# Scores ahead of up-sums on TensorE, and the dot product ahead of the gate product on VectorE, in two transformer blocks with 16,384 gathered experts

## The chip, the cores and the metric

The kernel runs on one core of a Trainium2 chip. The metric is the device time of that core in microseconds (us), for the whole program: two blocks of a transformer for 512 tokens of width 1024, in float32.

## What is computed

Two blocks follow one another. Each is a mixer (attention-like branches, merged by gates) and then a PEER feed-forward layer. That layer is what fills the time. Cut to what matters here:

```python
def peer_ffn(h, ...):
    q = h @ w_query                          # 8 heads, two halves of 128
    v1, i1 = top_k(q1 @ keys1, 16); v2, i2 = top_k(q2 @ keys2, 16)
    expert_idx, gates = ...                  # top 16 of the pairs, softmax: 8 * 16 = 128 experts a token
    u = take(expert_down, expert_idx)        # a row of 1024 for each token and expert
    act = gelu(einsum('bpd,bphkd->bphk', h, u))
    vv = take(expert_up, expert_idx)         # another row of 1024
    return einsum('bphk,bphkd->bpd', gates * act, vv)
```

The second block's mixer has three attentions (with a forget gate, with a sliding window and sinks, and over a memory of 256 tokens), whose items are scores, softmax and a weighted sum of values:

```python
s = einsum('bqhd,bkhd->bhqk', q_i, k) * scale + bias
p = softmax(where(mask, s, NEG_INF))
o = einsum('bhqk,bkhd->bqhd', p, v)
```

## The kernel before, in words

Tokens stand in tiles of 128, one token on each partition. For each of the 2 layers x 4 tiles x 128 experts, 1024 **slots** in all, one indirect DMA (L243, issued by POOL) gathers 128 rows of 8 KB, one for each token: the expert's down row and up row side by side, 1 MB, into one of 8 buffers (called held_z and held_pair in the profile: four of the buffers lie in the tile z). A slot n then passes through these steps:

- VectorE forms the **dot product** of the down rows with h (L309, a custom operation with a small read of the accumulator behind it) into `dot`.
- For two slots at a time (GROUP = 2), ScalarE makes **gelu** (L282, `bent`), and VectorE the **product of gelu and gate** (L304, `weight`).
- ScalarE makes a **diagonal** of the weight (L289, `diag`, one of 4 tiles), and TensorE multiplies the up rows by it and adds up over a tile's 128 slots in PSUM: the **up-sum** (L263, four matmuls, eight records in the profile).
- The end of the up-sum frees the buffer, and POOL issues the gather of slot n + 8 into it (L241 and L242 wait for `added`).

All this is cut into **beats**. In beat n, VectorE has the dot product of slot n and, for odd n from 3 on, the weights of the pair n - 3 and n - 2; ScalarE has gelu for the pair n - 2 and n - 1 if n is even, then the diagonal of slot n - 3; TensorE has the up-sum of slot n - 4; POOL issues slot n + 4. The order within a beat and engine is that in which the methods `pe`, `act` and `dve` of the class Gather write it (L252 to L329).

The beats run beside all the work that is left once the first tile's experts are chosen (host work, here): each stage takes `beats`, shares them out over its own steps, and calls `beats.pe(pe, step)` and its like on each engine after that step's own work. Host stages are the projections (p2, pg, po: TensorE mostly), head norms (hn), merges (mg), the choice of experts for the next tiles (c, with top-k on VectorE), and the attention stage (`attention_stage`, L843, foxa), which runs once for each half of the tokens. After about 3400 us only the drain is left: beats with nothing beside them.

`attention_stage` runs a software pipeline over N = 40 items, in N + 4 steps. In step s, TensorE has the scores of item s (`score`, L910, for the forget-gate items a second matmul L912) into one of two PSUM tiles, the transposes of item s - 2 (`turn`, L920), the weighted values of item s - 3 (`weigh_values`, L929) and then the step's beats. VectorE has the maximum of item s (`peak`, L984 to L988), which waits for the scores, the division for item s - 1 (`weigh`, L994 to L996), the copy of the result of item s - 4 (`take`, L1001) and then the beats. ScalarE has the exponential of item s (L952), the copy of the transposed item s - 2 (L965) and then the beats. Scores of item s wait until the exponential of item s - 2 has been made, since they use its PSUM tile.

The same function also serves an attention of the first block without beats ("mlaa"); there the order of instructions stays as it was.

Of the kernel before, what the change touches and what calls it, by code (L numbers as in the profile page):

```python
# [9 lines left out]
ALU = mybir.AluOpType  # L10
# [7 lines left out]
TT = S // P  # L18
# [21 lines left out]
NJ = PH * K16  # L40
# [169 lines left out]
class Gather:  # L210
# [85 lines left out]
                act.activation(self.sums[:, u * 512:(u + 1) * 512], self.acc[u][:], ACT.Copy).then_inc(self.kept, 1)  # L296

    def dve(self, dve, n):
        g, s = divmod(n - WEIGH_AT, GROUP)
        if s == 0 and 0 <= g < SLOTS // GROUP:  # L300
            t, q = divmod(g, NJ // GROUP)
            at = slice(q * GROUP, (q + 1) * GROUP)
            dve.wait_ge(self.bent_made, g + 1)
            dve.tensor_tensor(self.weight[:, t % 2, at], self.bent[:, t % 2, at], self.gate[:, t % TT, at], ALU.mult).then_inc(self.weighed, 1)  # L304
        if n < SLOTS:
            t, s = divmod(n, NJ)
            down = self.pair[n % BUFS][:, 0:D]
            dve.wait_ge(self.landed[n % BUFS], 16 * (n // BUFS) + 16)
            ins = dve.tensor_tensor_reduce(down, down, self.hrow[:, t % TT, :], 1.0, 0.0, ALU.mult, ALU.add, self.dot[:, t % 2, s:s + 1])  # L309
            if n % GROUP == GROUP - 1:  # L310
                ins.then_inc(self.dotted, 1)
        for u in range(2):
            t = self.tile_end(n, 3 + 2 * u)
            if t is not None:
# [528 lines left out]
def attention_stage(nc, name, k, items, heads, vdim, oT, sunk_from=None, sinks=None, sunk_T=None, sunk_loads=(), loads=(), saves=(), beats=None, spare=(), fetch=None,  # L843
# [21 lines left out]
    with ExitStack() as stack:  # L865
# [12 lines left out]
        with nc.Block(no_gpsimd_drain=True) as block:  # L878
# [20 lines left out]
            def _(pe):  # L899
# [23 lines left out]
                def weigh_values(n):  # L923
                    vs, (at, size, _, _) = items[n][3], lands(n)
                    pe.wait_ge(copied, n + 1)
                    if n >= 2 or n and not apart(n):
                        pe.wait_ge(taken, n - 1 if apart(n) else n)
                    for j, v in enumerate(vs):
                        last = pe.matmul(po[n % PO][at:at + size, 0:P], v, pT[n % 2][:, j * P:(j + 1) * P],  # L929
                                         start=j == 0, stop=j == len(vs) - 1)  # L930
                    last.then_inc(summed, 1)

                for step in range(N + 4):
                    if step < N:
                        score(step)
                    if 2 <= step < N + 2:
                        turn(step - 2)
                    if 3 <= step < N + 3:
                        weigh_values(step - 3)
                    beats.pe(pe, step)  # L940

            @block.scalar
# [1425 lines left out]
```

## Time and profile before

| | |
|---|---|
| median of 3 runs | 3985.33 us (3980.39 to 3996.19) |
| the profiled execution | 3991.26 us |
| its span, first to last instruction | 3989.4 us |
| first gather issued | 807.82 us |
| PE / DVE / ACT / POOL busy | 77% / 59% / 23% / 29% of the span |
| HBM read | 1256.17 MB, of it 1073.81 MB on the gathers' queue |
| granted TensorE clock, mean | 0.83 |

A row of the profile's windows gives, for a stretch of time in us from the span's start, the busy time of each engine with its number of instructions, then the granted TensorE clock as a share of full speed, the share of the stretch in which the 16 DMA engines were busy, and what they moved in GB/s. A row of waits names who waited, for whom, how long in total, how often, and the longest. In a row of the timeline the number in brackets is the idle time of that engine before the instruction, and what ended it. PE is TensorE, PEld its weight loads, DVE VectorE, ACT ScalarE.

### The profile page before, as it was taken

The page shows a single profiled execution, that of the slowest core. Times are in us where ns is not written, and L with a number is a line of the kernel's source. Part 1 is how long each engine was busy: PE and PEld are TensorE (multiplying, and loading weights), DVE is VectorE, ACT ScalarE, POOL GpSimd, SP SyncE. Part 2 cuts the span into 40 slices and gives each one's busy share as a digit, 9 for nine tenths or more (in the row PEclk, how much of TensorE's full clock was granted, in tenths as well). Part 3 has the DMA queues.
Part 4 walks back from the last instruction along what each step waited for, and adds up shares of the span by engine and source line. Part 5 has one row for each costly group of instructions (what it writes and reads, how often), then busy time and mean ns, then how long its engine had stood idle before and what let it go on. Part 6 is the DMA issues. An engine that isn't in the chain of part 4 may idle for free. (4 is left out here: it accounts for less than half of the span.)

```text
span 3989.4 us, 51160 instructions
## 1 busy us (share of the span) xinstructions
PE 3057.4 (77%) x18686; PEld 1577.7 (40%) x18686; DVE 2370.5 (59%) x6158; ACT 915.4 (23%) x2506; POOL 1152.4 (29%) x1029
## 2 busy tenths in 40 slices
PE   5975596756787765988899865979798876676666
PEld 4853395612354211633455522634465531111111
DVE  6557745476446677457545577457645578655554
ACT  2113232012111112136321111136412111111111
POOL 0000000043333444323323342323333334444442
PEclk8998698867798876977999986969999987766666
DMA  5510002289999999988999997977999999999998
GB/s 214 188 68 1 6 4 93 97 364 400 350 384 372 419 411 393 400 322 309 367 398 373 370 406 269 411 286 264 348 416 376 360 398 395 413 419 417 420 420 354
DMA packets 207064, 1263.90 MB, mean 317 GB/s; under 512 B 25748, under 2 KB 28948, under 8 KB 72356
## 3 DMA queue, kind: packets, MB, share of 16 engines
q0 software_dynamic: 147456, 1073.81, 67.3%
q1 hardware_dynamic: 59368, 186.95, 12.6%
q8 instruction: 143, 2.34, 0.2%
q14 instruction: 97, 0.79, 0.1%
HBM read 1256.17 MB, written 4.46 MB: 316 GB/s over the span
## 5 line engine op out<-in xcount | busy, mean ns | idle before, releaser
L243 POOL DMA_INDIRECT held_z<-in_experts,held_expert x512 | 579.0, 1131 | 1274.6 <-PE held_acc L263 907.6
L263 PE MATMUL held_acc<-held_z,held_diag 64*64 64x512 f32 x4096 | 697.6, 775 | 286.8 <-ACT held_diag L289 262.9
L263 PE MATMUL held_acc<-held_pair,held_diag 64*64 64x512 f32 x4096 | 688.9, 768 | 253.8 <-ACT held_diag L289 248.9
L243 POOL DMA_INDIRECT held_pair<-in_experts,held_expert x512 | 569.6, 1112 | 1047.6 <-PE held_acc L263 971.4
L309 DVE CUSTOM_DVE_ANT_0 held_z<-held_z,held_hrow 128x1024 f32<-128x1024 f32 x512 | 625.5, 1223 | 377.4 <-DMA held_z<-in_experts,held_expert 371.1
L309 DVE CUSTOM_DVE_ANT_0 held_pair<-held_pair,held_hrow 128x1024 f32<-128x1024 f32 x512 | 625.4, 1223 | 369.3 <-DMA held_pair<-in_experts,held_expert 360.7
L289 ACT ACTIVATE held_diag<-held_bands,held_weight 128x64 f32<-128x64 f32 x1024 | 347.7, 340 | 1467.7 <-DVE held_weight L304 1434.3
L263 PEld LDWEIGHTS held_acc<-held_z,held_diag 64*64 64x64 f32 x4096 | 135.2, 157 | 693.3 <-ACT held_diag L289 566.4
L263 PEld LDWEIGHTS held_acc<-held_pair,held_diag 64*64 64x64 f32 x4096 | 134.3, 155 | 670.4 <-ACT held_diag L289 570.8
L282 ACT ACTIVATE held_bent<-held_dot 128x2 f32<-128x2 f32 x512 | 104.0, 203 | 716.1 <-DVE held_dot L309 688.7
L1773 PE MATMUL c_ps<-held_hT,c_w 128*128 128x256 f32 x640 | 151.9, 392 | 0.0
L1250 POOL TENSOR_TENSOR rsolve_decays<-rsolve_ident,rwkv_dend 128x2048 f32<-128x2048 f32 x1 | 3.6, 3612 | 487.2 <-DMA rsolve_ident<-in_id 487.2
L645 PE MATMUL pgh_ps<-held_hT,pgh_w 128*128 128x256 f32 x608 | 141.2, 385 | 3.0 <-DMA pgh_w<-in_w_in 3.0
L1773 PEld LDWEIGHTS c_ps<-held_hT,c_w 128*128 128x128 f32 x640 | 121.8, 195 | 41.1 <-issue 25.1
L645 PE MATMUL p2h_ps<-held_hT,p2h_w 128*128 128x256 f32 x576 | 133.9, 386 | 0.0
L645 PEld LDWEIGHTS pgh_ps<-held_hT,pgh_w 128*128 128x128 f32 x608 | 112.4, 190 | 46.1 <-issue 27.6
L645 PEld LDWEIGHTS p2h_ps<-held_hT,p2h_w 128*128 128x128 f32 x576 | 106.5, 190 | 42.3 <-issue 29.2
L1817 DVE COPY held_z<-c_ps 128x256 f32<-128x256 f32 x64 | 27.2, 425 | 153.2 <-PE c_ps L1773 153.2
L546 PE MATMUL p_ps<-p_hhi,p_whi 128*128 128x512 f32 x272 | 107.9, 397 | 13.2 <-DVE p_wlo L565 13.2
L1773 PE MATMUL c_ps<-held_hT,held_z 128*128 128x256 f32 x384 | 99.0, 416 | 22.9 <-PEq L427 22.9
L547 PE MATMUL p_ps<-p_hlo,p_whi 128*128 128x512 f32 x272 | 106.8, 393 | 0.0
L548 PE MATMUL p_ps<-p_hhi,p_wlo 128*128 128x512 f32 x272 | 106.7, 392 | 0.0
(499 smaller groups left out, 4038.8 us busy)
## 6 DMA issues: line engine op xcount, KB each, us to landing
pgh_w<-in_w_in SPq DMA_DIRECT2D x38, 512.0 KB
p2h_w<-in_w_in SPq DMA_DIRECT2D x36, 512.0 KB
p_raw<-in_w_in SPq DMA_DIRECT2D x34, 512.0 KB, 3.5
p_w_ada<-in_w_ada SPq DMA_DIRECT2D x16, 1024.0 KB, 6.1
c_w<-in_w_query SPq DMA_DIRECT2D x20, 512.0 KB, 3.2
held_z<-in_w_in SPq DMA_DIRECT2D x20, 512.0 KB
c_w<-in_w_peer_q SPq DMA_DIRECT2D x20, 512.0 KB
ada_w<-in_w_ada SPq DMA_DIRECT2D x4, 2048.0 KB, 18.7
```

Of the source, the lines that this page charges most:

```text
L243: pool.indirect_dma_start(self.pair[m % BUFS], None, self.layers[t // TT][0], bass.IndirectOffsetOnAxis(ap=self.expert[:, t % TT, s:s + 1] ...
L263: last = pe.matmul(self.sum_of(i)[to * BAND:(to + 1) * BAND], diag[band, :], up[band, turn * WIDE:(turn + 1) * WIDE], start=s == 0, stop=s ...
L282: act.activation(self.bent[:, t % 2, at], self.dot[:, t % 2, at], self.layers[t // TT][1]).then_inc(self.bent_made, 1)
L289: act.activation(self.diag[m % DIAGS][:], self.k.bands[:], ACT.Copy, scale=self.weight[:, t % 2, s:s + 1]).then_inc(self.diag_made, 1)
L309: ins = dve.tensor_tensor_reduce(down, down, self.hrow[:, t % TT, :], 1.0, 0.0, ALU.mult, ALU.add, self.dot[:, t % 2, s:s + 1])
L546: pe.matmul(out, hi, hhi[:, c, :], start=c == 0, stop=False)
L547: pe.matmul(out, hi, hlo[:, c, :], start=False, stop=False)
L548: last = pe.matmul(out, lo, hhi[:, c, :], start=False, stop=c == kc - 1)
L645: last = pe.matmul(ps[n % 4][:, 0:tokens], w[n % WEIGHT_TILES][:, c, :], act_in[:, c, :], start=c == 0, stop=c == kc - 1)
L1250: pool.tensor_tensor(decays[:], bcast(ident[:], RP * S // CH, 1), bcast(dend[:], CH, 2), ALU.mult).then_inc(decays_made, 1)
L1773: last = pe.matmul(ps[n % 2][:, 0:tokens], w[n % W][:, c, :], hT[:, c, :], start=c == 0, stop=c == DC - 1)
L1817: dve.tensor_copy(qT[:, n, :], ps[n % 2][:, 0:tokens]).then_inc(used, 1)
```

## The change

Two edits, and no instruction more or less. In a beat of VectorE the dot product of slot n now stands in front of the product for the pair n - 3 and n - 2. In the attention stage, TensorE has the scores of item 0 ahead of the loop, and in step s the scores of item s + 1 behind that step's weighted values and in front of its beats. The queues of ScalarE, POOL and SP are as before.

```diff
     def dve(self, dve, n):
-        g, s = divmod(n - WEIGH_AT, GROUP)
-        if s == 0 and 0 <= g < SLOTS // GROUP:
-            t, q = divmod(g, NJ // GROUP)
-            at = slice(q * GROUP, (q + 1) * GROUP)
-            dve.wait_ge(self.bent_made, g + 1)
-            dve.tensor_tensor(self.weight[:, t % 2, at], self.bent[:, t % 2, at], self.gate[:, t % TT, at], ALU.mult).then_inc(self.weighed, 1)
         if n < SLOTS:
             t, s = divmod(n, NJ)
             down = self.pair[n % BUFS][:, 0:D]
...
             if n % GROUP == GROUP - 1:
                 ins.then_inc(self.dotted, 1)
+        g, s = divmod(n - WEIGH_AT, GROUP)
+        if s == 0 and 0 <= g < SLOTS // GROUP:
+            t, q = divmod(g, NJ // GROUP)
+            at = slice(q * GROUP, (q + 1) * GROUP)
+            dve.wait_ge(self.bent_made, g + 1)
+            dve.tensor_tensor(self.weight[:, t % 2, at], self.bent[:, t % 2, at], self.gate[:, t % TT, at], ALU.mult).then_inc(self.weighed, 1)
...
+                score(0)
                 for step in range(N + 4):
-                    if step < N:
-                        score(step)
                     if 2 <= step < N + 2:
                         turn(step - 2)
                     if 3 <= step < N + 3:
                         weigh_values(step - 3)
+                    if step + 1 < N:
+                        score(step + 1)
                     beats.pe(pe, step)
```

On VectorE, in the last beats of the drain, before the change (ISA is the dot product and the read of its accumulator; held_landed6 is the semaphore of buffer 6's gather):

```order
L309 ISA held_pair6,held_dot<-held_pair6,held_hrow 128x1024 [waits held_landed6]
L309 ISA held_dot 128x1
L304 TENSOR_TENSOR held_weight<-held_bent,held_gate 128x2 [waits held_bent_made]
L309 ISA held_pair7,held_dot<-held_pair7,held_hrow 128x1024 [waits held_landed7]
L309 ISA held_dot 128x1
```

and after it, where the two operations have the lines 303 and 311:

```order
L303 ISA held_pair6,held_dot<-held_pair6,held_hrow 128x1024 [waits held_landed6]
L303 ISA held_dot 128x1
L303 ISA held_pair7,held_dot<-held_pair7,held_hrow 128x1024 [waits held_landed7]
L303 ISA held_dot 128x1
L311 TENSOR_TENSOR held_weight<-held_bent,held_gate 128x2 [waits held_bent_made]
```

The weights of a pair now stand behind two dot products in a row, and so behind the wait for the second one's gather.

On TensorE, two steps of the first attention stage among the sliding-window items, before (foxah0_ps are the score tiles, pt the transposes, po the weighted values, held_acc the up-sums):

```order
L910 MATMUL foxah0_ps0<-partsh0_swa_k,held_z 128x128
L920 MATMUL foxah0_pt0<-held_ident,held_z 128x128 x2
L929 MATMUL foxah0_po0<-foxah0_p0,partsh0_v 64x128
L263 MATMUL held_acc0<-held_z,held_diag2 64x512
L263 MATMUL held_acc1<-held_z,held_diag2 64x512
L263 MATMUL held_acc0<-held_z,held_diag2 64x512
L263 MATMUL held_acc1<-held_z,held_diag2 64x512
L910 MATMUL foxah0_ps1<-partsh0_swa_k,held_z 128x128
```

and after:

```order
L920 MATMUL foxah0_pt0<-held_ident,held_z 128x128 x2
L929 MATMUL foxah0_po0<-foxah0_p0,partsh0_v 64x128
L910 MATMUL foxah0_ps1<-partsh0_swa_k,held_z 128x128
L263 MATMUL held_acc0<-held_z,held_diag2 64x512
L263 MATMUL held_acc1<-held_z,held_diag2 64x512
L263 MATMUL held_acc0<-held_z,held_diag2 64x512
L263 MATMUL held_acc1<-held_z,held_diag2 64x512
L920 MATMUL foxah0_pt1<-held_ident,held_z 128x128 x2
```

The scores into tile ps1 have moved over one up-sum of four matmuls, towards the front.

## Rows read from the trace of the kernel before

**Rows 1.** The page: TensorE's busy time, and the DMA engines' share in 40 slices.
```profile
PE 3057.4 (77%) x18686; PEld 1577.7 (40%) x18686; DVE 2370.5 (59%) x6158; ACT 915.4 (23%) x2506; POOL 1152.4 (29%) x1029
...
DMA  5510002289999999988999997977999999999998
```

**Rows 2.** Windows: all beats; the second and third choice of experts; the drain.
```profile
812.00:3984.00 3172.00, 2472.25 (x12820) 1103.15 (x12820) 1898.36 (x5147) 717.95 (x2127) 1145.28 (x1021) 0.82 0.94 377
1206.60:1579.00 372.40, 259.04 (x1449) 102.78 (x1449) 265.06 (x825) 64.14 (x221) 161.88 (x138) 0.81 0.99 403
2214.00:2466.30 252.30, 179.28 (x976) 84.88 (x976) 189.28 (x664) 41.67 (x133) 89.94 (x79) 0.83 0.92 364
3400.00:3984.00 584.00, 397.02 (x1864) 66.85 (x1864) 305.83 (x601) 94.69 (x352) 238.00 (x224) 0.66 0.99 409
```

**Rows 3.** Waits from 822 to 3984 us: diagonals for weights, dot products for gathers.
```profile
ACT held_diag L289 <- DVE held_weight L304: 1434.3, 438, 16.6
...
DVE held_z L309 <- DMA held_z<-in_experts,held_expert: 365.1, 279, 3.1
DVE held_pair L309 <- DMA held_pair<-in_experts,held_expert: 360.7, 275, 4.0
```

**Rows 4.** What ended VectorE's idle time before the 512 products of L304.
```profile
  ACT held_bent L282: 15.4, 10
```

**Rows 5.** Timeline in the drain: one buffer, from gather to gather.
```profile
3882.93 0.94 POOL L243 DMA_INDIRECT held_z<-in_experts,held_expert  x1 [1.99 <-PE held_acc L263]
...
3893.87 1.23 DVE L309 CUSTOM_DVE_ANT_0 held_z<-held_z,held_hrow 128x1024 f32<-128x1024 f32 x1 [1.27 <-DMA held_z<-in_experts,held_expert]
...
3900.01 0.16 DVE L304 TENSOR_TENSOR held_weight<-held_bent,held_gate 128x2 f32<-128x2 f32 x1
3900.20 0.35 ACT L289 ACTIVATE held_diag<-held_bands,held_weight 128x64 f32<-128x64 f32 x1 [2.13 <-DVE held_weight L304]
...
3900.60 1.98 PE L263 MATMUL held_acc<-held_z,held_diag 64*64 64x512 f32 x8 [0.50 <-ACT held_diag L289]
3901.35 1.22 DVE L309 CUSTOM_DVE_ANT_0 held_z<-held_z,held_hrow 128x1024 f32<-128x1024 f32 x1 [1.19 <-DMA held_z<-in_experts,held_expert]
...
3902.88 0.94 POOL L243 DMA_INDIRECT held_z<-in_experts,held_expert  x1 [1.54 <-PE held_acc L263]
...
3913.82 1.23 DVE L309 CUSTOM_DVE_ANT_0 held_z<-held_z,held_hrow 128x1024 f32<-128x1024 f32 x1 [1.27 <-DMA held_z<-in_experts,held_expert]
```

**Rows 6.** Timeline: the first gather of all, and its dot product.
```profile
807.82 1.11 POOL L243 DMA_INDIRECT held_z<-in_experts,held_expert  x1 [316.59 <-DVE held_expert L1677]
...
813.48 1.23 DVE L309 CUSTOM_DVE_ANT_0 held_z<-held_z,held_hrow 128x1024 f32<-128x1024 f32 x1 [3.45 <-DMA held_z<-in_experts,held_expert]
```

**Rows 7.** Windows: narrow items of both attention stages; wide items of the second.
```profile
1840.00:1948.80 108.80, 82.94 (x471) 33.37 (x470) 85.29 (x272) 74.08 (x179) 43.83 (x35) 0.89 0.87 325
2674.00:2754.00 80.00, 79.21 (x331) 30.65 (x332) 46.52 (x127) 46.72 (x88) 20.40 (x17) 0.82 0.63 225
2754.00:2854.00 100.00, 81.82 (x491) 35.66 (x493) 82.70 (x258) 71.25 (x168) 36.28 (x32) 0.93 0.86 315
```

**Rows 8.** VectorE's waits, 1840 to 1948.8 us: for scores, and the first for gathers.
```profile
DVE foxah_ps L984 <- PE foxah_ps L910: 6.8, 6, 2.1
DVE foxah_nmax L985 <- PE foxah_ps L910: 4.6, 4, 1.4
DVE held_z L309 <- DMA held_z<-in_experts,held_expert: 4.3, 2, 3.1
```

**Rows 9.** VectorE's longest wait for scores, 2754 to 2860.3 us.
```profile
DVE foxah_ps L984 <- PE foxah_ps L910: 5.5, 4, 2.1
```

**Rows 10.** TensorE's wait for diagonals, 1840 to 1948.8 us.
```profile
PE held_acc L263 <- ACT held_diag L289: 10.1, 9, 2.4
```

**Rows 11.** Timeline in the first attention stage: an up-sum, and the scores behind it.
```profile
1846.84 1.09 PE L263 MATMUL held_acc<-held_pair,held_diag 64*64 64x512 f32 x8
...
1847.86 0.48 PE L910 MATMUL foxah_ps<-partsh_swa_k,held_z 64*128 64x128 f32 x2
```

## The prediction

> **What bounds the kernel now.** I read the page first, then the windows, then the waits, then the timeline. On the page TensorE is the busiest engine, but from about the ninth slice the DMA digits are nearly all 9 [rows 1]. The windows make that exact: over the 3172 us of beats the DMA engines are busy for a share of 0.94, in the second choice of experts 0.99, in the drain 0.99 [rows 2]. So most of this part goes at the pace of the gathers, and all that any reordering can win is 0.06 x 3172 = 190 us. In the waits, ScalarE waits 1434 us for weights, but behind that stands VectorE, whose dot products wait 365.1 + 360.7 = 726 us for gathers [rows 3]. The first is a shadow of the second. It becomes a price only if buffers come free too late for the DMA engines to stay busy. That is the question for the one edit. The other edit acts in the two attention stages alone, where the DMA share is 0.87 and 0.86 among the narrow items and 0.63 among the wide ones [rows 7].
>
> **The dot product in front of the weights, DMA-bound stretches.** I follow one buffer in the drain [rows 5]. Its gather is issued at 3882.93, its dot product starts at 3893.87, the pair's weights are made at 3900.01 at the end of the dot product before, the diagonal at 3900.20, the up-sum from 3900.60 to 3902.58, and the next gather into it is issued at 3902.88, whose dot product starts at 3913.82. From dot product to next issue are 9.01 us, from issue to dot product 10.94, together 19.95 us for a ring of 8 buffers, 2.49 us a gather.
>
> With the change the weights stand behind the next dot product too, which waits 1.19 us for its gather and starts at 3901.35, lasting 1.22 us: so the weights come at about 3902.57 rather than 3900.01, 2.5 us later. The even slot's buffer comes free 2.5 us later. The odd one's up-sum then queues behind the even one's (1.98 us at half clock, 1.09 at full clock, [rows 5, 11]), so it is 1 to 2.3 us late as well. What does 2.5 us cost? The 10.94 us from issue to dot product are mostly queueing. The first gather of all, issued with nothing ahead of it, had its dot product 813.48 - 807.82 = 5.66 us later [rows 6]. So the ring needs 9.01 + 2.5 + 5.66 = 17.2 us, and has 19.95. There are 2.8 us to spare, the DMA engines stay fed, and the drain's 584 us do not change: **0 us**.
>
> The Trainium skill (DMA: Bandwidth & Descriptors, the section on the anatomy of one DMA on the gpsimd path) gives about 2.0 us plus the bytes over 436 GB/s for such a DMA. As an estimate from that page, 1 MB is 4.4 us, which would leave 4.0 us to spare and the same 0 us in the sum. Our row, 5.66 us, is longer, and the sum uses the row.
>
> In the three choices of experts with beats beside them VectorE's top-k and TensorE's projections come between the beats, so a slot's way is longer and uneven. The second choice has 372.40 us for 138 gathers, 2.70 us each, a ring of 21.6 us [rows 2]. Against the 17.2 us needed, 4.4 us are left for such host work. That covers the usual case, not the worst. The rows show no operation that tells how often it is not enough. Bounds: 0 below (a gain is excluded but for the 15.4 us in which the product had waited for gelu [rows 4], and VectorE isn't the bound here), and above 2.5 us for every tenth of about 150 pairs, some 40 us. The nearest row, the drain with its 2.8 us of room, speaks for the low end. I take **+4 us**.
>
> At the end of a stage whose last beat is odd, the product (0.16 us) and the last diagonal (0.35 us [rows 5]) now stand behind the last dot product rather than beside it. There are 29 stages with beats, half of them odd: 14 x 0.5 = 7 us if each were bare. In DMA-bound stages the queued gathers cover it. I take **+2 us**, bounds 0 and +7.
>
> **The scores in front of the up-sums.** Only the order on TensorE moves; no DMA is issued or passed. Scores of item s + 1 need the exponential of item s - 1. The weighted values in front of them already wait for a ScalarE copy that stands behind that exponential, so no new wait arises. What is won is VectorE's wait for scores. Among the wide items TensorE is busy 79.21 of 80 us [rows 7]: there order wins nothing, **0 us**. Among the narrow ones VectorE is busy 85.29 of 108.80 and 82.70 of 100 us, and most of the rest are short steps between dependent instructions. It waits there for scores 6.8 + 4.6 = 11.4 us, 10 times, in the first stage [rows 8]. In the second the first of these rows has 5.5 us, 4 times [rows 9], and the other is the same to the digit, so 10.1 us, 8 times. That is 1.1 to 1.3 us each, and an up-sum that now comes later lasts 1.09 us [rows 11], so nearly all of the 21.5 us could go. The ceiling is the DMA: (1 - 0.87) x 108.8 = 14.1 and (1 - 0.86) x 100 = 14.0 us. Part of what VectorE no longer waits for scores it will wait for gathers, as it already does there for 4.3 us. I take three quarters, **-16 us**, bounds 0 and -28.
>
> TensorE's own waits for diagonals, 10.1 us in the first stage's narrow part [rows 10], pull both ways. The up-sum stands 0.48 to 0.9 us later, behind the scores, but the weights come at least one dot product, 1.22 us, later. They may grow by half a us each, but the scores no longer stand behind them, so VectorE doesn't feel it: 0 us, bounds 0 and +10. Up-sums later by a score free their buffers later too. With a DMA share of 0.87 and a VectorE that is behind its gathers, that is covered; if VectorE caught up, gathers would be late next.
>
> **Sum.** -16 + 4 + 2 = -10 us against the profiled execution's 3991.26, so 3981. That execution lay 5.9 us above the median of 3985.33, so the median should be **3975 us**.
>
> **Rivals.**
>
> *The attention stages reach the DMA's pace*, the likely wrong side if I am too careful. Both narrow parts win the full 14 us each, and the product that no longer stands in front of a dot product takes gelu's lateness (15.4 us in all [rows 4]) off VectorE's path, for some 5 us of it. -28 - 5 + 3 = -30, so 3955 us. For it: VectorE's idle time there is short. Against: the waits removed must all lie on the path.
>
> *The ring starves*, the case on the slow side. In the choices of experts the weights wait for the next gather, the buffers come free 2.5 us later, the gathers are issued later, and the dot product that is waited for comes later itself. Place: 1206 to 1579, 2214 to 2466 and 3123 to 3400 us, about 315 gathers. It decides from the point at which the time from issue to dot product falls to 5.7 us for a good part of the slots. Price: the +40 us above, less 10 won: 4015 us. For it: the second window already has a DMA share of 0.92 [rows 2], so its ring does run dry at times. Against: the 2.8 and 4.4 us of room. The Trainium skill (TensorE: Matmul & The Clock Gate, on engine queue depths) says that VectorE's queue is strictly first in, first out. By that rule the product cannot pass the waiting dot product. Before, the 512 products never waited for a gather, but only 15.4 us for gelu [rows 4].
>
> *The score edit does nothing that is seen*: DVE's waits for scores come back under another name (for gathers, or for TensorE's values), and the losses cancel the rest: 3985 to 3990 us.
>
> **Chances.** A measurement of this kernel can tell about 0.5%, 20 us, from no change. My forecast of a small gain 0.45, the attention stages at the DMA's pace 0.27, nothing seen 0.15, the ring starves 0.13. Faster by over 0.5% (below 3965) 0.27, within 0.5% 0.60, slower by over 0.5% 0.13. The forecast's own range is 3966 to 3985. The range for 8 in 10 takes in most of the fast case and the low part of the slow one: 3950 to 4006.
>
> **What would show it.** In the changed profile, each product should start right behind the dot product of an odd slot rather than an even one, and in the drain the up-sums should come in pairs, with a gather every 2.49 us still and a share of 0.99. The time from issue to dot product in the drain should fall from 10.9 to about 8.5 us. VectorE's waits for scores in the narrow parts should fall from 11 us to under 4 in each stage, the two narrow parts should be about 8 us shorter each, and the wide parts as long as before. I am wrong if the drain is longer than 584 us or its DMA share falls, if the choices of experts take over 10 us more in all, or if the attention stages keep their length though the waits for scores are gone.

## The result, and the profile after

The changed kernel takes 4060.68 us (median of 4 runs, 4056.61 to 4067.59), beside 3984.64 us for the kernel before: a ratio of 1.0183 (95% interval 1.0157 to 1.0209). It is slower by 76 us. 3975 us was forecast, 3950 to 4006 with a chance of 8 in 10, and 0.13 for slower by over 0.5%.

Its profiled execution has a span of 4065.8 us, 76.4 more than before. Its page, against [rows 1, 3]: the engines' busy time, the DMA digits, and two groups (busy time and mean ns | idle time in front, what ended it).

```profile
PE 3009.4 (74%) x18686; PEld 1606.6 (40%) x18686; DVE 2368.3 (58%) x6158; ACT 874.2 (22%) x2506; POOL 1175.8 (29%) x1029
...
DMA  5510003299999999989999897977999889999998
...
L289 ACT ACTIVATE held_diag<-held_bands,held_weight 128x64 f32<-128x64 f32 x1024 | 347.9, 340 | 2327.8 <-DVE held_weight L311 2327.2
...
L1818 DVE COPY held_z<-c_ps 128x256 f32<-128x256 f32 x64 | 27.2, 425 | 246.2 <-PE c_ps L1774 246.2
```

No engine has more instructions, and none but POOL (1175.8 for 1152.4 us) is busy for longer; the DMA engines have lost some of their 9s. ScalarE's wait for weights grew from 1434.3 to 2327.2 us, 893 us for a loss of 76: as large a shadow as in [rows 3]. The row that counts most is the last. It is VectorE's copy of a projection of the router's query (`c_ps`, 4 choices x 16 chunks), and the same row before the change read:

```profile
L1817 DVE COPY held_z<-c_ps 128x256 f32<-128x256 f32 x64 | 27.2, 425 | 153.2 <-PE c_ps L1773 153.2
```

93 us more of waiting, by the engine on which everything else in these stages hangs. VectorE's first step on a tile's key scores (`c_scores`, the other thing that TensorE makes for the choice) shows the same. Before and after:

```profile
L1614 DVE MAX8 c_v<-c_scores 128x8 f32<-128x128 f32 x128 | 31.7, 290 | 13.3 <-PE c_scores L1604 12.3
```

```profile
L1615 DVE MAX8 c_v<-c_scores 128x8 f32<-128x128 f32 x128 | 31.8, 290 | 44.0 <-PE c_scores L1605 43.1
```

Such sums are signs and no prices: with the score edit alone (experiment 1) the copy waits 180.1 us in one profile and 159.0 in a second, with choices as long as before within 5 us.

The fourth choice up to the drain before the change, and then windows of the changed kernel for the second and third choice of experts, the fourth up to the drain, and the drain:

```profile
3123.50:3400.00 276.50, 203.73 (x1128) 89.74 (x1128) 196.43 (x676) 45.35 (x155) 108.32 (x98) 0.83 0.98 392
```

```profile
1219.10:1620.20 401.10, 260.39 (x1448) 109.31 (x1448) 263.98 (x825) 56.91 (x219) 151.58 (x138) 0.82 0.95 375
2242.80:2517.70 274.90, 190.78 (x976) 90.60 (x976) 188.84 (x664) 37.62 (x132) 88.87 (x79) 0.77 0.85 331
3171.40:3476.00 304.60, 215.57 (x1128) 96.83 (x1128) 197.34 (x682) 40.34 (x155) 107.42 (x97) 0.79 0.91 356
3476.00:4060.00 584.00, 329.93 (x1872) 76.96 (x1864) 304.70 (x595) 82.58 (x353) 267.80 (x224) 0.76 0.99 408
```

Against [rows 2] the second choice went from 372 to 401 us and its DMA share from 0.99 to 0.95, the third from 252 to 275 and from 0.92 to 0.85, the fourth from 277 to 305 and from 0.98 to 0.91. Each held the same number of gathers, within one. The drain is the same 584 us at 0.99, though its up-sums now come in pairs behind one diagonal wait, sixteen records in a row:

```profile
3892.39 1.95 PE L263 MATMUL held_acc<-held_pair,held_diag 64*64 64x512 f32 x16 [1.51 <-ACT held_diag L289]
```

The program's stages, from the first instruction of one to the first of the next in the traces, in us. "Again" is a second profile of the changed kernel; the last column is the score edit alone (two profiles).

| stage | before | changed | again | scores alone |
|---|---|---|---|---|
| first choice | 238.3 | 242.8 | 242.6 | 237.0, 237.9 |
| second choice | 371.9 | 401.1 | 398.3 | 374.3, 371.0 |
| third choice | 251.9 | 274.9 | 274.8 | 256.6, 255.9 |
| fourth choice and drain | 865.9 | 894.4 | 895.4 | 864.9, 866.4 |
| first attention stage | 169.8 | 154.8 | 152.4 | 146.7, 146.8 |
| second attention stage | 186.2 | 181.3 | 175.7 | 173.9, 174.4 |

The four choices lose 85 us (83 in the second profile), the two attention stages win 20 (28). All other stages together differ by 11 us, 6 of them from before the first gather, where the change has done nothing yet (0.5 in the second profile).

Of the choices' 85 us, 59 lie in the parts with the projections of the second, third and fourth choice (18, 21 and 20 us). In these three parts the mean time from one copy of a projection to the next went from 8.60 to 9.80, from 7.14 to 8.48 and from 7.26 to 8.48 us: some 1.2 to 1.3 us a step, about the 1.22 us of one dot product. The first choice has beats beside its second tile only, and loses 4.5 us.

### The profile page after: what moved, and what is told of

It is laid out like the page before. It is cut to its first block and busy times, and to the rows that moved or that the text cites. A ratio compares the mean times of both kernels' runs of the same rounds, so it can differ in the third digit from the quotient of the medians.

```text
span 4065.8 us, 51160 instructions
## 1 busy us (share of the span) xinstructions
PE 3009.4 (74%) x18686; PEld 1606.6 (40%) x18686; DVE 2368.3 (58%) x6158; ACT 874.2 (22%) x2506; POOL 1175.8 (29%) x1029
## 5 line engine op out<-in xcount | busy, mean ns | idle before, releaser
L263 PE MATMUL held_acc<-held_z,held_diag 64*64 64x512 f32 x4096 | 655.0, 746 | 361.5 <-ACT held_diag L289 344.6
L243 POOL DMA_INDIRECT held_pair<-in_experts,held_expert x512 | 589.1, 1151 | 1050.5 <-PE held_acc L263 975.3
L263 PE MATMUL held_acc<-held_pair,held_diag 64*64 64x512 f32 x4096 | 658.8, 752 | 314.9 <-ACT held_diag L289 314.9
L289 ACT ACTIVATE held_diag<-held_bands,held_weight 128x64 f32<-128x64 f32 x1024 | 347.9, 340 | 2327.8 <-DVE held_weight L311 2327.2
L263 PEld LDWEIGHTS held_acc<-held_pair,held_diag 64*64 64x64 f32 x4096 | 144.0, 155 | 700.1 <-ACT held_diag L289 560.9
L1774 PE MATMUL c_ps<-held_hT,c_w 128*128 128x256 f32 x640 | 154.6, 397 | 0.0
L645 PE MATMUL p2h_ps<-held_hT,p2h_w 128*128 128x256 f32 x576 | 133.9, 386 | 0.0
L1774 PE MATMUL c_ps<-held_hT,held_z 128*128 128x256 f32 x384 | 112.2, 457 | 22.9 <-PEq L427 22.9
L1774 PEld LDWEIGHTS c_ps<-held_hT,held_z 128*128 128x128 f32 x384 | 88.0, 235 | 59.0 <-issue 43.5
```

The source lines that it names most:

```text
L243: pool.indirect_dma_start(self.pair[m % BUFS], None, self.layers[t // TT][0], bass.IndirectOffsetOnAxis(ap=self.expert[:, t % TT, s:s + 1] ...
L263: last = pe.matmul(self.sum_of(i)[to * BAND:(to + 1) * BAND], diag[band, :], up[band, turn * WIDE:(turn + 1) * WIDE], start=s == 0, stop=s ...
L289: act.activation(self.diag[m % DIAGS][:], self.k.bands[:], ACT.Copy, scale=self.weight[:, t % 2, s:s + 1]).then_inc(self.diag_made, 1)
L645: last = pe.matmul(ps[n % 4][:, 0:tokens], w[n % WEIGHT_TILES][:, c, :], act_in[:, c, :], start=c == 0, stop=c == kc - 1)
L1774: last = pe.matmul(ps[n % 2][:, 0:tokens], w[n % W][:, c, :], hT[:, c, :], start=c == 0, stop=c == DC - 1)
```

## Where the choices lose it: one loop through two queues

Waits over the second choice, before (who waited, for whom, us in total, times, longest):

```profile
ACT held_diag L289 <- DVE held_weight L304: 193.0, 63, 6.9
...
DVE held_z L1817 <- PE c_ps L1773: 35.8, 15, 5.1
DVE held_pair L309 <- DMA held_pair<-in_experts,held_expert: 33.1, 33, 2.3
DVE held_z L309 <- DMA held_z<-in_experts,held_expert: 31.3, 31, 2.0
```

and after:

```profile
ACT held_diag L289 <- DVE held_weight L311: 318.4, 69, 8.7
...
DVE held_z L1818 <- PE c_ps L1774: 73.1, 16, 6.7
...
DVE held_pair L303 <- DMA held_pair<-in_experts,held_expert: 26.8, 22, 3.7
...
DVE held_z L303 <- DMA held_z<-in_experts,held_expert: 20.2, 23, 1.3
```

VectorE waits 37 us more for projections and 17 us **less** for gathers. So late gathers are not what slowed VectorE here. The timeline of one step shows the way. Before:

```profile
1265.95 0.42 DVE L1817 COPY held_z<-c_ps 128x256 f32<-128x256 f32 x1 [2.93 <-PE c_ps L1773]
...
1269.03 1.22 DVE L309 CUSTOM_DVE_ANT_0 held_z<-held_z,held_hrow 128x1024 f32<-128x1024 f32 x1 [0.17 <-issue]
...
1270.18 0.15 DVE L304 TENSOR_TENSOR held_weight<-held_bent,held_gate 128x2 f32<-128x2 f32 x1
...
1270.78 1.09 PE L263 MATMUL held_acc<-held_z,held_diag 64*64 64x512 f32 x8 [2.54 <-ACT held_diag L289]
...
1271.79 3.72 PE L1773 MATMUL c_ps<-held_hT,c_w 128*128 128x256 f32 x16
...
1275.55 0.43 DVE L1817 COPY held_z<-c_ps 128x256 f32<-128x256 f32 x1 [2.84 <-PE c_ps L1773]
```

The same step after the change:

```profile
1285.21 0.42 DVE L1818 COPY held_z<-c_ps 128x256 f32<-128x256 f32 x1 [3.71 <-PE c_ps L1774]
...
1288.29 1.23 DVE L303 CUSTOM_DVE_ANT_0 held_z<-held_z,held_hrow 128x1024 f32<-128x1024 f32 x1 [0.17 <-DVE c_idx L1623]
...
1289.44 1.22 DVE L303 CUSTOM_DVE_ANT_0 held_z<-held_z,held_hrow 128x1024 f32<-128x1024 f32 x1
...
1290.59 0.16 DVE L311 TENSOR_TENSOR held_weight<-held_bent,held_gate 128x2 f32<-128x2 f32 x1
...
1291.18 1.99 PE L263 MATMUL held_acc<-held_z,held_diag 64*64 64x512 f32 x8 [3.69 <-ACT held_diag L289]
...
1293.10 5.33 PE L1774 MATMUL c_ps<-held_hT,c_w 128*128 128x256 f32 x16
...
1298.46 0.42 DVE L1818 COPY held_z<-c_ps 128x256 f32<-128x256 f32 x1 [6.58 <-PE c_ps L1774]
```

Follow the releasers round. The copy lets VectorE go on to top-k, dot products and weight; the weight gives the diagonal; the up-sum waits for the diagonal; **the next projection stands behind the up-sum in TensorE's queue** though it needs nothing from it; the next copy waits for the projection. From copy to copy it was 9.60 us and is 13.25. The 3.65 us are: 1.15 for the second dot product in front of the weight, 0.91 for an up-sum that takes 1.99 instead of 1.09 us, 1.60 for a projection that takes 5.33 instead of 3.72 us. In the last two the granted clock shows. From the start of the up-sum to the end of the projection it was 1.00 before the change, and after it:

```profile
1291.18:1298.46 7.28, 7.28 (x28) 4.53 (x32) 0.71 (x2) 0.28 (x2) 0.94 (x1) 0.64 0.97 399
```

It stood at 0.5 of full speed, the lower level of 1.2 GHz, from 1289.56 to 1296.39 us, and fell there while TensorE was idle: for 3.69 us in front of this up-sum, before the change for 2.54.

That one step is not typical in these two terms: 3.65 us, where the mean step grew by 1.2 to 1.3. Over all four choices the projection's matmuls (1024 records) grew from 151.9 + 99.0 to 154.6 + 112.2 us, 16 us, and the up-sums in the parts with projections by 8 us, at a granted clock of 0.89 to 0.90 there for 0.94 to 0.97 before. So of the 59 us in these parts up to 24 can be the clock. How much of that lies on the loop's path no run separates.

## The experiments

All of them are timed against the kernel before on the same chip.

**1. The score edit alone** (VectorE in its old order).

```diff
+                score(0)
                 for step in range(N + 4):
-                    if step < N:
-                        score(step)
...
+                    if step + 1 < N:
+                        score(step + 1)
                     beats.pe(pe, step)
```

> The score edit alone; VectorE's order as in the kernel before. The two attention stages were 14.9 and 4.9 us shorter in the changed kernel, everything else that moved was in the choices of experts. Both theories (a loop between VectorE and TensorE in the choices; the ring of buffers running dry there) put all of the loss on the other edit, so both expect 3985 - 20 = 3965 us, 0.995 of before. If the choices stay longer than before by more than 5 us each, the loss is not the dot product's alone.

Measured: 3961.73 us (3957.85 to 3964.86), ratio 0.9935 (0.9914 to 0.9956). A gain of 26 us. The choices are not shorter than before (4.7 us longer in this profile), the attention stages are, by 35 us. A second profile of the same kernel:

> The kernel with the attention-score edit alone, profiled a second time. In its first profile the wide items of the second attention stage took 57.3 us at a granted clock of 0.83, in the changed kernel 64.5 us at 0.73, with TensorE busy all of the time in both. If that is the order of VectorE's instructions, 57 us again. If it is the run, either value can come.

Measured: 3961.52 us (one run). It gave the same stages within some 3 us, and 56.9 us at 0.84 for those wide items. That alone would have spoken for VectorE's order; experiments 5 and 10 speak against it.

**2. The dot-product edit alone** (TensorE in its old order).

```diff
-        g, s = divmod(n - WEIGH_AT, GROUP)
...
         if n < SLOTS:
...
+        g, s = divmod(n - WEIGH_AT, GROUP)
```

> The dot product ahead of the weights alone; TensorE's order as in the kernel before. If the edits add up: 4061 + 20 = 4081 us, with all three choices longer by 23 to 30 us as in the changed kernel, and the attention stages within 3 us of before. If the attention stages got their gain from both edits together, they are longer than before here.

Measured: 4099.38 us (4093.13 to 4107.11), ratio 1.0286 (1.0262 to 1.0310), a loss of 112 us, more than was expected. The second, third and fourth choice are longer by 28, 23 and 29 us, as in the changed kernel. The attention stages took 167.8 and 196.1 us, for 169.8 and 186.2 before; the 9.9 us in the second are outside what was expected, and 9.2 of them lie among its wide items (71.0 us at a granted clock of 0.70, for 61.8 at 0.79). Experiments 1 and 2 add up to 86, near the 76 of both together. All of the loss is this edit's.

**3. The old VectorE order in the choices of experts only**, the new one everywhere else.

```diff
+    gather.weights_first = True
     chunks = 2 * PH
...
+                    gather.weights_first = False
```

> The changed kernel, but with the weights ahead of the dot product again in the query stages (projection of queries and choice of experts), by a flag that the stage sets. If the loss sits wholly in these stages: 3965 us, as with the scores alone, and the drain is 584 us, though it has the new order. If the ring theory holds for the rest too (the attention stages, projections and drain near their limit): above 3975 us.

Measured: 3978.51 us (3969.61 to 3987.93), ratio 0.9975 (0.9964 to 0.9986). 82 us of the changed kernel's time come back. The place of most of the loss is shown: it is the choices (the first 238.4, the second 371.0, the third 255.5, the fourth with the drain 867.5 us), and not the drain. But it is not all of it. 3978.51 us is above the line of 3975 drawn beforehand, and 17 us above experiment 1 (3961.73), whose interval lies wholly below this one's. From there this kernel differs only by the new order outside the choices. So the new order costs something there too. Against experiment 1 the profile (27 us longer) has 11 us in the attention stages and 16 in the stages other than choices and attention. Which wait they go through was not followed up.

**4. Why there: the projection ahead of the beats.** The changed kernel, VectorE's order left as changed; only TensorE's next projection moves in front of the up-sums, so that it no longer waits behind the late diagonal. This tells the loop from the starved ring, for the weights come as late as ever.

```diff
+                project(0)
                 for n in range(chunks):
...
+                    if n + 1 < chunks:
+                        project(n + 1)
                     beats.pe(pe, n)
```

> The changed kernel, and in the query stages TensorE has the projection of chunk n + 1 ahead of the up-sums of chunk n's beats (the PSUM tile and the copy that it waits for are free by then). Loop theory: an up-sum that waits for late weights no longer holds up the projection, VectorE's 246 us of waiting for projections (153 before) fall below 100, and most of the 18 to 20 us lost in each of the three projection parts comes back: 4061 - 50 = 4010 us or less. Ring theory: the up-sums come later still by a projection of 3.1 to 5.3 us, buffers come free later, and it gets slower: 4070 to 4100 us.

Measured: 4006.7 us (3999.51 to 4018.73), ratio 1.0046 (1.0028 to 1.0064): 54 us came back by an edit that does nothing to the weights. Its window and waits over the second choice:

```profile
1220.60:1604.20 383.60, 261.30 (x1448) 107.47 (x1448) 265.04 (x825) 56.90 (x219) 158.30 (x138) 0.80 0.98 392
```

```profile
ACT held_diag L289 <- DVE held_weight L311: 308.5, 68, 7.4
...
DVE held_pair L303 <- DMA held_pair<-in_experts,held_expert: 50.4, 39, 4.2
...
DVE held_z L303 <- DMA held_z<-in_experts,held_expert: 39.4, 35, 2.6
DVE c_v L1615 <- PE c_scores L1605: 17.3, 9, 3.1
```

ScalarE waits for weights nearly as long as before this edit (308.5 and 318.4 us), so the weights are about as late; yet the stage is 17 us shorter. The wait for projections is gone from the list, VectorE waits for gathers again (89.8 us), and the DMA share is back at 0.98. The parts with projections are as short as before the change (132.0, 110.8 and 111.2 us, for 133.9, 113.5 and 114.4). A row for key scores stands in the list: 17.3 us for `c_scores`, which still stand behind the up-sums. That is the same loop through another step, and it led to the next run.

**5. The key scores ahead too.**

```diff
-                        if i < LISTED:
-                            choice.scores(pe, j, at, i)
+                        if i + 1 < LISTED:
+                            choice.scores(pe, j, at, i + 1)
...
                         later.pe(pe, PIECES * (j - 1) + i)
```

> The changed kernel; in the choices of experts TensorE has the next projection ahead of each beat (as in the run before) and now the next key scores of the second, third and fourth tile's choice ahead of its beats as well. Loop theory: what was left of the loss in the choices (the first 244.6 against 238.3 us, the second 383.7 against 371.9) is the same loop through the key scores, so the two come down by 4 and 8 us and the kernel to 3990 to 3999 us. Rival, late weights cost by themselves in these pieces (buffers free too late): 4002 to 4012 us, as without it.

Measured: 3983.34 us (3976.57 to 3995.77), ratio 0.9983 (0.9969 to 0.9997). Another 23 us, more than expected. The first choice is at 239.6 us, the second at 381.0, the wait for key scores is no longer listed (15.2 us in the whole kernel, for 52.1 in experiment 4). The two profiles are 37 us apart: some 16 us lie in the choices, and 9 in the attention stages and 11 in all other stages, which this edit doesn't touch. So a part of the 23 is the run. Its wide items of the second attention stage took 57.3 us, at a granted clock of 0.83, with VectorE in its new order.

**6. The same with VectorE's old order** (the edits of 1, 4 and 5 together), to see whether there is more to be had.

> The kernel before with the attention-score edit alone, plus projections and key scores ahead of the beats on TensorE; VectorE in its old order. Loop theory: with the old order the loop is shorter than the gathers' pace wherever the DMA share is 0.99, so only the third choice (share 0.92, 252 us) and the fourth can win: 3950 to 3964 us. Rival, TensorE's order matters to the choices in itself: below 3945 us. Rival, up-sums that stand later free buffers later: above 3970 us.

Measured: 3957.88 us (3945.55 to 3967.54), ratio 0.9907 (0.9876 to 0.9938). With the old order there is little to be had: experiment 1 (0.9914 to 0.9956) can't be told from this. That tests a rival, that TensorE's order saves the same time whatever VectorE does. In part it does: its parts with projections take 412 us in all four choices, for 430 to 435 with the score edit alone, so the loop was there in the old order too. But with the new order the same edits took them from 485 to 418 us.

Experiments 5 and 6 differ only in VectorE's order. With TensorE's own work ahead it costs 3983 - 3958 = 25 us, where it had cost 4061 - 3962 = 99. In the profiles it costs the choices 20 us, where it had cost them 80. So three quarters of the price go through TensorE's queue; the last 20 us in the choices stay open.

Experiments 1 and 6 are the fastest kernels of the study, faster than the one before and than the changed one.

**7 and 8. The ring's arithmetic, with 6 buffers instead of 8.** The prediction said that the ring had 2.8 us to spare. Two buffers fewer take the room away.

```diff
-GROUP, BUFS, DIAGS = 2, 8, 4
+GROUP, BUFS, DIAGS = 2, 6, 4
```

> The kernel before with 6 buffers for gathers instead of 8. It tests the ring arithmetic of the prediction: the ring needs 9.01 + 5.66 = 14.7 us, for 6 buffers 2.44 us a gather, just under the 2.49 us that the DMA engines take. So the drain (224 gathers) should take 584 to 600 us. Should the 5.66 us of a lone gather be too short a figure for one with others beside it, it is longer than 620 us.

> The changed kernel with 6 buffers instead of 8. The ring needs 9.01 + 2.5 + 5.66 = 17.2 us, for 6 buffers 2.87 us a gather: the drain should take 224 x 2.87 = 640 us, some 50 us more than with the order before, where with 8 buffers the two were equal. If the late weights do not lengthen a buffer's way, the two kernels with 6 buffers have the same drain, within 5 us.

Measured: 4428.52 us in the old order, 4751.17 in the new (one run each). The drains, from the dot product of slot 800 to that of slot 1023, first in the old order and then in the new:

```profile
3763.50:4408.00 644.50, 410.74 (x1796) 66.48 (x1792) 294.65 (x570) 89.20 (x336) 240.83 (x222) 0.58 0.96 363
```

```profile
3983.40:4729.90 746.50, 392.20 (x1796) 86.55 (x1788) 294.40 (x570) 76.60 (x335) 252.51 (x222) 0.62 0.87 314
```

With 8 buffers the same stretch takes 561.0 and 560.5 us. Both expectations were too low, 644.5 for 584 to 600 and 746.5 for 640. From the issues and dot products of slots 800 to 999, means in us:

| buffers, order | a gather every | issue to dot | dot to next issue |
|---|---|---|---|
| 8, old | 2.51 | 11.10 | 8.94 |
| 8, new | 2.51 | 9.36 | 10.68 |
| 6, old | 2.90 | 7.54 | 9.83 |
| 6, new | 3.36 | 6.92 | 13.20 |

Two things were wrong. The first is the way from issue to dot product. 5.66 us is near the shortest there is (5.5 and 5.4 us the lowest with 6 buffers), but with others under way the mean is 7.5 and 6.9.

The second is that the way from dot product to next issue is no constant: a slot's diagonal stands behind the dot products of later slots, and each of these comes at the gathers' own pace. In the old order both slots of a pair wait for the slot two further on. The diagonals start 1.4 us after the start of that one's dot product: for the first slot because the weight stands behind it, for the second because in ScalarE's queue the gelu of the next pair, which waits for it, stands in front of the diagonal. In the new order the first slot of a pair waits for the slot three further on (1.3 us after its start), and the second for the one two further on, as before (1.7 us). So there are 2 paces in the way in the old order, and 2.5 on average in the new. What is left is 8.94 - 2 x 2.51 = 3.9 and 9.83 - 2 x 2.90 = 4.0 us; 10.68 - 2.5 x 2.51 = 4.4 and 13.20 - 2.5 x 3.36 = 4.8 us, nearly the same for 6 and 8 buffers. So the edit does not cost 2.5 us of a ring, it takes **one buffer** away from every second slot, and 0.5 to 0.8 us from each on top.

The pace is then (4.0 + 7.5) / (6 - 2) = 2.9 us in the old order and (4.8 + 6.9) / (6 - 2.5) = 3.3 in the new. That only writes the table's rows another way and is no test. With 8 buffers, as an estimate from the same figures, the least pace of the new order would be (4.8 + 6.9) / 5.5 = 2.1 us, below the 2.5 of the DMA engines, and the drain is unmoved.

**9. Filler work for the clock.** How much of the loop is the granted clock?

```diff
                         choice.scores(pe, 0, at0, n // 2 - 1)
+                    if 0 < n < chunks - 1:
+                        pe.wait_ge(used, n)
+                        for _ in range(8):
+                            pe.matmul(ps[(n + 1) % 2][:, 0:tokens], k.ident[:], hT[:, 0, :], start=True, stop=True)
                     beats.pe(pe, n)
```

> The changed kernel; in the choices of experts, behind each projection 1 to 14 and in front of the beats, TensorE makes 8 more matmuls of the identity with the hidden states, 128x256 each, into the PSUM tile that the next projection overwrites (some 1.9 us at full clock, 3.7 at half, 56 times; the output is unchanged). They lie in the time in which TensorE waits for the diagonal (3.69 us in one such beat), so they add nothing to the loop as long as they fit. If the clock is part of the loop's price (1.6 us of 3.7 a beat), the up-sum and the projection behind it run faster and the choices get shorter: 4010 to 4040 us against 4061. If the clock is only a bystander and the loop is priced by its dot product and its waits alone: 4055 to 4070. If the extra work lies on the loop and gives nothing back: 4080 to 4160.

Measured: 4146.9 us (4133.34 to 4148.52), ratio 1.0384 (1.0354 to 1.0414). The lines of its page for the filler and for the projections:

```profile
L1789 PE MATMUL c_ps<-held_hT,held_ident 128*128 128x256 f32 x896 | 202.6, 379 | 0.0
L1774 PE MATMUL c_ps<-held_hT,c_w 128*128 128x256 f32 x640 | 147.7, 384 | 0.0
L1774 PE MATMUL c_ps<-held_hT,held_z 128*128 128x256 f32 x384 | 98.1, 413 | 22.9 <-PEq L427 22.9
```

The filler was mis-sized: eight matmuls are 16 records and 202.6 / 56 = 3.62 us, twice what was written down, and fill the whole idle time even at full clock. And a quarter of it lies where there is no loop with up-sums: beside the first choice's projections there are no beats, and there the 14 fillers, 50.7 us, made the choice 50 us longer (293.0 for 242.8). In the other three choices 152 us of filler cost 34 us. The projections ran faster, 245.8 us where the changed kernel had 266.8, and the granted clock in their parts was 0.98 to 0.99, where it had been 0.89 to 0.90. At nearly full clock these parts are still longer than in the changed kernel: work of TensorE in front of the up-sum is in part paid for in this loop. It does not tell what the clock alone is worth; that stays open, at up to the 24 us above.

**10. The changed kernel, profiled again.**

> The changed kernel, profiled a second time. The losses by stage should come again within some 5 us: second choice of experts 29 us longer than before the change, third 23, fourth with the drain 28. The wide items of the second attention stage: 64.5 us at 0.73 again if the order of instructions decides it, 57 or 64 us if it is the run.

Measured: 4054.64 us. The choices' losses came again within 3 us each (table above), and those of their parts with projections within 1 us (60 for 59). The wide items of the second attention stage took 57.3 us at 0.83, not 64.5 at 0.73: the next part needs that.

## The attention stages

Windows over the wide and the narrow items of the first attention stage, then of the second (from the first item's maximum to the 13th's, and on to the 40th's). Before:

```profile
1780.20:1833.90 53.70, 51.20 (x196) 19.72 (x188) 31.62 (x100) 29.63 (x68) 14.65 (x13) 0.62 0.80 307
1833.90:1933.00 99.10, 79.88 (x436) 32.23 (x436) 80.87 (x264) 74.31 (x175) 38.97 (x32) 0.90 0.87 320
2677.70:2739.50 61.80, 61.30 (x252) 23.50 (x244) 36.24 (x99) 35.60 (x69) 15.14 (x13) 0.79 0.62 219
2739.50:2844.80 105.30, 88.14 (x502) 37.74 (x500) 85.31 (x264) 77.69 (x174) 36.48 (x31) 0.94 0.83 301
```

With the score edit alone (experiment 1):

```profile
1780.70:1821.40 40.70, 40.70 (x194) 16.41 (x193) 31.47 (x99) 29.65 (x67) 12.75 (x12) 0.78 0.94 368
1821.40:1908.20 86.80, 77.21 (x434) 31.42 (x437) 80.63 (x265) 73.63 (x174) 39.57 (x31) 0.90 0.94 368
2659.90:2717.20 57.30, 57.30 (x244) 21.80 (x246) 36.50 (x99) 35.96 (x69) 14.94 (x12) 0.83 0.62 222
2717.20:2812.40 95.20, 86.30 (x506) 37.07 (x502) 85.40 (x264) 77.34 (x173) 36.86 (x31) 0.95 0.89 328
```

And the changed kernel:

```profile
1824.30:1869.80 45.50, 45.44 (x192) 17.85 (x192) 31.44 (x99) 30.33 (x67) 13.44 (x12) 0.69 0.86 326
1869.80:1958.80 89.00, 78.04 (x438) 31.25 (x438) 80.53 (x265) 74.12 (x171) 40.49 (x31) 0.90 0.93 355
2729.00:2793.50 64.50, 64.50 (x244) 24.63 (x246) 36.40 (x99) 36.22 (x69) 15.77 (x12) 0.73 0.56 201
2793.50:2887.90 94.40, 84.79 (x506) 36.59 (x502) 85.34 (x264) 77.58 (x170) 36.46 (x31) 0.96 0.88 325
```

The narrow items are 10.1 and 10.9 us shorter in the changed kernel, 12.3 and 10.1 with the score edit alone. The surprise is the first stage's wide items, 53.7 us before and 45.5 or 40.7 after. Their waits, before the change and in experiment 1:

```profile
DVE foxah_ps L984 <- PE foxah_ps L912: 21.9, 11, 3.1
```

```profile
DVE foxah_ps L985 <- PE foxah_ps L912: 7.7, 6, 2.1
```

TensorE was busy for 51.2 of 53.7 us there, which reads like a bound, but at a granted clock of 0.62. Multiply: 51.20 x 0.62 = 31.7 and 40.70 x 0.78 = 31.7. The work is the same to the digit; it was done at a lower clock. Of the profiles taken of this stage, the two with TensorE's old order (the kernel before and experiment 2) have 53.7 and 53.1 us at 0.62 and 0.60, the nine with its new order 40.6 to 45.5 us at 0.69 to 0.78. So the order is the cause of the gain. That the clock rose because TensorE no longer stands idle there (2.5 us before, 0.0 in experiment 1) fits the rows, but no run shows it apart from the order.

## Why the prediction was wrong

- **The choices of experts, +4 us (bounds 0 and +40): the step that failed.** They lose 83 to 85 us, experiment 3, with the old order there, gives 82 us back, and some three quarters of the price go through TensorE's queue (experiments 4 to 6). The prediction followed one buffer through its ring, and asked only whether gathers would be late. It never asked what else stands behind an up-sum that waits. On TensorE the host stage's own projection does (in the code it is issued right in front of the beats of its step, so behind those of the step before), and VectorE waits for that projection in front of everything. The row was there to be read: the copy's 153.2 us of idle time before the change, 35.8 of them in the second choice, were a sign of this loop already. "4.4 us are left for such host work" mistook work that is part of a loop for work that is covered.
- **The rival on the slow side** named the right place and the wrong mechanism. In the second choice VectorE waited less for gathers, 47 for 64 us, not more, and experiment 4 took 54 us back with the weights about as late as ever. The lower DMA share was mostly a consequence, no cause: in experiment 4 it is back at 0.98. Its +40 was too low for the same reason. For the rule of the Trainium skill that went with it (TensorE: Matmul & The Clock Gate, on engine queue depths), that VectorE's queue is strictly first in, first out, the trace agrees: in the drain the weights' product, which by then had all that it reads but had to stand behind the second dot product's wait, came 8.7 us after its pair's first dot product, where it had come after 6.2. But the queue that cost the time was TensorE's.
- **The drain, 0 us: right.** 584.00 us and a share of 0.99, up-sums in pairs. The 8.5 us forecast from issue to dot product are 9.4 on average, for 11.1 before. From dot product to next issue it is 2.1 us more for the first slot of a pair and 1.4 more for the second, near the 2.5 and the 1 to 2.3 that were forecast. The reason given was half right: the room is there, but it is counted in paces, not in us (experiments 7 and 8). That the drain came out at 0 was in part luck: with 8 buffers there was enough room by either count.
- **The narrow items, -16 us: right in kind, too small.** They won 21 us, and VectorE's waits for scores fell from 11.5 and 13.0 us to 2.6 and 4.2. The ceiling of 14 us a stage that I took from the DMA share held in each.
- **The wide items, 0 us: wrong in the first stage.** I read the second stage's row [rows 7], where TensorE was busy for 79.21 of 80 us, and took it for both. In the second stage the order did win nothing that stands out of the clock's own scatter; in the first it won 8 to 13 us.
- **TensorE's waits for diagonals in the attention stages, 0 us:** the same kernel with and without VectorE's new order differs by 8 and 7 us in the two stages, 6 and 1 in the second profiles, most of it among the wide items. The 15 us of the first profiles are outside the bounds of 0 and +10, the 7 of the second inside. The waits themselves did not grow: among the narrow items they fell from 10.5 and 10.0 us to 5.8 and 5.2.
- **Stage ends, +2 us:** no row shows them by themselves. All stages from the first choice on, other than the choices and the attention, are together 5 and 8 us longer in the two profiles. In the four other profiles of kernels with VectorE's new order there (experiments 2 to 5) they are 5 to 17 us longer, in the three with the old one -3 to +1. So something is paid there, more than 2 us, and whether it is stage ends stays open.

The sum, for the two profiles of the changed kernel: 85 - 20 + 11 = 76 us and 83 - 28 + 8 = 63 us, the amounts by which their spans are longer than that of before.

## What to carry to other kernels

Before you put anything in front of a result that another engine waits for, list what stands **behind that wait** in the waiting engine's queue, and look whether one of those instructions feeds the engine you are editing. If so it is a loop, and each us that you add is paid once a turn, however idle both engines look. The mend is cheap: issue the independent work of the waiting engine ahead of its wait (here moving the projection gave back 54 of the 99 us that the new order had cost, and the key scores another 23). And count the room of a ring of buffers in turns: for each slot whose release waits for one more later slot, the ring is one buffer shorter.

## What the runs showed of the hardware

- The same instructions, with TensorE busy in every us of them, took 57.3 us at a granted clock of 0.83 in one profile of the changed kernel and 64.5 us at 0.73 in another (wide items, second attention stage). Of seven further profiles of kernels with the same TensorE order there, four had 0.83 or 0.84 and three 0.73. That is a scatter of 7 us in a stage that no edit explains.
- TensorE's busy time times its granted clock stayed at 47 to 48 us in that stretch (61.30 x 0.79, 57.30 x 0.83, 64.50 x 0.73), and at 31 to 32 in the first stage's. Here the product follows the work, where busy time alone does not.
- Behind 3.69 us of idleness, in which the granted clock fell to 0.5, an up-sum took 1.99 us and the projection behind it 5.33. Behind 2.54 us, at 1.0 throughout, they took 1.09 and 3.72.
- A gather of 1 MB that starts alone reached its dot product after 5.66 us. With 6 buffers, and so others under way, the means were 7.5 and 6.9 us at DMA shares of 0.96 and 0.87, the lowest 5.5 and 5.4.
